# A block inversion whose last level works on 64-row quadrants, and a sample-state product split over two 32-row groups

## What is computed

```python
a = jnp.where(strict, beta[..., :, None] * jnp.einsum('bnhid,bnhjd->bnhij', k, k) * decay, 0.0)
lhs = a + jnp.eye(CHUNK)
sol = lax.linalg.triangular_solve(lhs, rhs, left_side=True, lower=True, unit_diagonal=True)
...
s = gl_c[..., None, None] * s + jnp.einsum('bhcd,bhce->bhde', ko_c, u)
```

## Time and profile before

| | us |
|---|---|
| median of 3 runs (1190.07 to 1191.61) | 1191.23 |
| the profiled execution | 1191.59 |
| its span | 1189.5 |
| PE busy | 1148.7 (97%) |
| DVE, POOL, ACT busy | 726.2, 610.2, 518.5 |
| one phase of the loop (two successive starts of line 778: 297.87 and 374.17) | 76.30 |
| mean granted TensorE clock | 0.99 |

### The profile page before, as it was taken

How to read it: one execution, slowest core, us unless ns; L and a number is a source line. 1 busy time by engine, 2 the same in 40 slices (tenths; PEclk the granted TensorE clock), 3 DMA queues, 4 the chain that set the end, 5 groups by cost and what they waited for, 6 DMA issues and landing times.

```text
span 1189.5 us, 22147 instructions
## 1 busy us (share of the span) xinstructions
PE 1148.7 (97%) x8349; PEld 1096.0 (92%) x8349; DVE 726.2 (61%) x1064; ACT 518.5 (44%) x898; POOL 610.2 (51%) x480
## 2 busy tenths in 40 slices
PE   6789999999999999999999989999999999999996
PEld 5689989899899998999989979999999999999996
DVE  6678896886868868778683546764135215314735
ACT  6554545544445354553462576542133123213531
POOL 0338558386584764847657374332433433435841
PEclk9899999999999999999999999999999999999998
DMA  6211223112222122121321116212222222222212
GB/s 236 61 57 45 75 73 100 57 35 81 74 72 83 31 85 74 50 78 44 98 93 41 49 38 222 71 54 72 77 83 90 73 87 88 71 88 89 91 35 80
DMA packets 32519, 92.28 MB, mean 78 GB/s; under 512 B 4688, under 2 KB 12240, under 8 KB 32464
## 3 DMA queue, kind: packets, MB, share of 16 engines
q1 hardware_dynamic: 32464, 91.52, 23.7%
HBM read 82.99 MB, written 8.52 MB: 77 GB/s over the span
## 4 chain that ended last, share of the span: by engine, by line
PE 77%; DVE 11%; issue 6%; ACT 4%; POOL 1%; DMA 0%; DVEq 0%; SPq 0%; ACTq 0%; POOLq 0%
PE ps L529 29%; PE ps L558 23%; PE ps L567 6%; DVE work L1338 5%; PE ps L883 4%; DVE ps L1341 4%; PE ps L716 2%; PE ps L696 2%; PE ps L711 2%; PE ps L770 1%; PE ps L778 1%; PE ps L744 1%; PE ps L577 1%; PE ps L590 1%; DVE o_a L1341 1%
## 5 line engine op out<-in xcount | busy, mean ns | idle before, releaser
L1812 POOL TENSOR_TENSOR w_lo<-raw,w_hi 128x1024 fp32r<-128x1024 f32 x123 | 298.6, 2429 | 380.3 <-ACT w_hi L981 225.8
L558 PE MATMUL ps<-in_hi,w_hi 128*128 128x288 f32 x992 | 305.7, 308 | 3.0 <-ACT work L1058 2.8
L558 PE MATMUL ps<-in_hi,w_lo 128*128 128x288 f32 x992 | 300.3, 303 | 0.0
L558 PE MATMUL ps<-in_lo,w_hi 128*128 128x288 f32 x992 | 299.0, 301 | 0.0
L558 PEld LDWEIGHTS ps<-in_hi,w_hi 128*128 128x128 f32 x992 | 188.9, 190 | 6.6 <-ACT w_hi L963 3.0
L558 PEld LDWEIGHTS ps<-in_hi,w_lo 128*128 128x128 f32 x992 | 188.9, 190 | 2.0
L558 PEld LDWEIGHTS ps<-in_lo,w_hi 128*128 128x128 f32 x992 | 188.8, 190 | 1.2
L1341 DVE SCALAR_TENSOR_TENSOR ps<-work,ct,ps 128x512 f32<-128x512 f32 x240 | 180.7, 753 | 7.4 <-DVE work L1460 1.7
L981 ACT CAST w_hi<-raw 128x1024 fp32r<-128x1024 f32 x61 | 63.8, 1047 | 224.3 <-PE ps L529 224.3
L1338 DVE TENSOR_TENSOR f_tmp<-f_tmp 128x576 f32<-128x576 f32 x31 | 70.7, 2282 | 96.4 <-ACT f_tmp L1288 91.0
L1338 DVE TENSOR_TENSOR o_a<-o_a,ps 128x576 f32<-128x576 f32 (+1 forms) x40 | 25.3, 634 | 144.7 <-PE ps L529 122.8
(11 more groups left out here) (290 smaller groups left out, 2396.0 us busy)
## 6 DMA issues: line engine op xcount, KB each, us to landing
raw<-w_all_in SPq DMA_DIRECT2D x136, 512.0 KB, 3.6
work<-s_in_in SPq DMA_DIRECT2D x8, 512.0 KB, 3.6
s_sample_out<-work SPq DMA_DIRECT2D x8, 512.0 KB, 2.7
xt<-x_t_in SPq DMA_DIRECT2D x4, 576.0 KB, 6.4
xt<-x_t_in SPq DMA_DIRECT2D x2, 1152.0 KB, 7.5
y_out<-o_a SPq DMA_DIRECT2D x16, 144.0 KB, 1.7
halo<-halos_in SPq DMA_DIRECT2D x9, 156.0 KB, 3.4
conf_rows_out<-c_rows SPq DMA_DIRECT2D x8, 135.0 KB, 2.2
```

Source lines behind the costliest of these rows:

```text
L558: t = mm(dense_ps(n, j, h), a[:, w, k], b[:, k, h * HALF:(h + 1) * HALF], start=r == 0, stop=r == PASS_MM // 2 - 1)
L1812: return gp.tensor_tensor(out, a, b, op)
```

## The change

The last level (l = 7) joins two 64-wide blocks of a 128-wide chunk. After the change only the quadrants that are not zero are computed:
- x: 4 matmuls of 64 weight columns and 64 moving columns over rows 0 to 63 (upper right quadrant of c, upper left of t). ACT copies the result, 64 partitions by 256 elements, to partitions 64 to 127 of `x_r`.
- u^T x and x^T u: 4 and 4 matmuls of the same size over rows 64 to 127. DVE writes the negated first result to a quadrant of `t_r` that was zero, and subtracts the second from the one quadrant of `u_r`.
- POOL copies one quadrant of the matrix to `c_r` instead of multiplying the whole with a mask.
- A `nop` on PE carries the waits ahead of the small groups, one on POOL ahead of its copy.

For the sample states `um` becomes 64x512, row r keeping the column block of sequence r // 8 mod 4. The two matmuls contract over rows 0 to 31 and 32 to 63, each into its own PSUM bank.

```diff
+        def quad(ap, i, j):
+            return ap[i * HP:(i + 1) * HP, 0:SEQ].rearrange("p (a b) -> p a b", a=TILES)[:, :, j * HP:(j + 1) * HP]
+
+        def sub(ap, c, i, j):
+            return ap[i * HP:(i + 1) * HP, c * P + j * HP:c * P + (j + 1) * HP]
...
+                        if l == LEVELS:
+                            pe.nop(nofuse=True)
                         for c in range(TILES):
-                            r = mm(tile(g(0), c), tile(w, c), tile(t, c),
-                                   start=True, stop=True)
+                            if l == LEVELS:
+                                r = mm(sub(g(0), c, 0, 0), sub(w, c, 0, 1), sub(t, c, 0, 0), start=True, stop=True)
+                            else:
+                                r = mm(tile(g(0), c), tile(w, c), tile(t, c), start=True, stop=True)
...
+                        if l == LEVELS:
+                            pe.nop(nofuse=True)
                         if l <= LEVELS:
                             for c in range(TILES):
-                                r = mm(tile(g(0), c), tile(u_r, c), tile(x_r, c), start=True, stop=True)
+                                if l == LEVELS:
+                                    r = mm(sub(g(0), c, 0, 0), sub(u_r, c, 1, 1), sub(x_r, c, 1, 0),
+                                           start=True, stop=True)
+                                else:
+                                    r = mm(tile(g(0), c), tile(u_r, c), tile(x_r, c), start=True, stop=True)
...
                         for c in range(TILES):
-                            r = mm(tile(g(1), c), tile(x_r, c), tile(u_r, c), start=True, stop=True)
+                            if l == LEVELS:
+                                r = mm(sub(g(1), c, 0, 1), sub(x_r, c, 1, 0), sub(u_r, c, 1, 1),
+                                       start=True, stop=True)
+                            else:
+                                r = mm(tile(g(1), c), tile(x_r, c), tile(u_r, c), start=True, stop=True)
...
                         for q in range(2):
-                            r = mm(g(q), smw(v["ko"]), v["um"][0:SMP, q * SEQ:(q + 1) * SEQ],
+                            rows = slice(q * SMP // 2, (q + 1) * SMP // 2)
+                            r = mm(g(q), v["ko"][rows, SEQ:SEQ + P], v["um"][rows, 0:SEQ],
                                    start=True, stop=True)
...
-                        r = A(x_r[:], g(0), ACT.Copy)
+                        if l == LEVELS:
+                            r = A(quad(x_r, 1, 0), quad(g(0), 0, 0), ACT.Copy)
+                        else:
+                            r = A(x_r[:], g(0), ACT.Copy)
...
-                        r = tt(t_r[:], t_r.bitcast(F32)[:, :], g(0), ALU.subtract)
+                        if l == LEVELS:
+                            r = ve.tensor_scalar(quad(t_r, 1, 0), quad(g(0), 0, 0), -1.0, None, ALU.mult)
+                        else:
+                            r = tt(t_r[:], t_r.bitcast(F32)[:, :], g(0), ALU.subtract)
...
-                    r = tt(dst, u_r.bitcast(F32)[:, :], g(1), ALU.subtract)
+                    if l == LEVELS:
+                        r = tt(quad(u_r, 0, 1), quad(u_r.bitcast(F32), 0, 1), quad(g(1), 0, 1), ALU.subtract)
+                    else:
+                        r = tt(dst, u_r.bitcast(F32)[:, :], g(1), ALU.subtract)
...
+                elif l == LEVELS:
+                    pool.nop(nofuse=True)
+                    r = gp.tensor_copy(quad(cr, 0, 1), quad(v["at"], 0, 1))
                 else:
                     r = tt(pr(cr), pr(v["at"]), lvl(l), ALU.mult)
...
-                        tt(v["um"][0:SMP, :].rearrange("p (q c) -> p q c", q=NS),
-                           smw(v["u"]).unsqueeze(1).to_broadcast([SMP, NS, P]),
-                           con("rowm", SMP).unsqueeze(2).to_broadcast([SMP, NS, P]),
+                        tt(v["um"][0:SMP, 0:SEQ].rearrange("p (q c) -> p q c", q=NS // 2),
+                           smw(v["u"]).unsqueeze(1).to_broadcast([SMP, NS // 2, P]),
+                           con("rowm", SMP).unsqueeze(2).to_broadcast([SMP, NS // 2, P]),
                            ALU.mult).then_inc(um_ready, 1)
...
-    put("rowm", np.arange(SMP)[:, None] // LS == np.arange(NS)[None, :])
+    put("rowm", np.arange(SMP)[:, None] // LS % (NS // 2) == np.arange(NS // 2)[None, :])
```

More of the change, by code:

```diff
@@ L32 @@
 P = 128
+HP = P // 2
 D = 1024
@@ L82 @@
            ("eps", 1), ("eps128", 1), ("big", P), ("big_s", SMP), ("lvl", LEVELS * P),
-           ("lvl_s", LEVELS_S * SMP), ("strict", P), ("rowm", NS)]
+           ("lvl_s", LEVELS_S * SMP), ("strict", P), ("rowm", NS // 2)]
 OFF, _o = {}, 0
```

## The result

| | before | after |
|---|---|---|
| median of all runs, us (12 each) | 1191.98 | 1185.44 |
| profiled execution's span, us | 1189.5 | 1182.2 |
| states of one phase to those of the next (372.49 less 297.01, before 374.17 less 297.87) | 76.30 | 75.48 |

The ratio of the times is 0.9950, 95% interval 0.9937 to 0.9964: **6.0 us faster**, between 4.3 and 7.5. I had said 3.6.

The account below looks back on a forecast made before the run. PE was taken as the bound, busy 1148.7 of 1189.5 us. Level 7 -0.2, states -3.0 and last head -0.4 sum to -3.6 us: 1188.0 against the profiled execution, 1187.6 as a median, range 1186.8 to 1191.2.

Parts of the forecast that it names:

- Bound by PE, and the saving reaches the end: Heads: PE and DVE both released by line 778, both start 0.43 us sooner, wait at line 684 unchanged.
- Level 7 nets nothing: Level 7: x group 0.07 to 0.12 us slower, slot 19 0.10 to 0.15 faster; -0.2 us over 8 heads.
- The switch: Level 7: leaving the full array for small matmuls and returning costs 0.30 to 0.35 us.
- The rival in which the 64-wide weights load no faster: Level 7: the 12 small matmuls keep 0.11 us spacing, costing +4.8 us; chance 0.05 as the slower rival.
- the slower case: Level 7's small matmuls keep 0.11 us spacing and the state halves queue: +4.4 us, 1195.6; chance 0.05.
- The states: Sample states: second matmul's first record beside the first's second, three spacings for four, 0.43 us a head.
- Seven heads: The sample-state gain of 0.43 us counts in seven heads, -3.0 us (0 to -3.0), lost in the last.
- The last head: Last head: half the `um` spreading saves POOL about 0.9 us, shortening PE's wait; -0.4 us (0 to -0.9).
- the level at +0.2: Level 7's term at the slow end of its bounds, -0.6 to +0.2 us over 8 heads.
- the case without overlap: Sample states: the two halves queue, only -0.2 and -0.4 us remain, 1190.6 us; chance 0.24.

Follow-up runs that it names:

- both halves in one row group: Changed kernel with both sample-state matmuls contracting over rows 0 to 31, rows 32 to 63 left out: 1.91 us to the sum, phase 76.26 us.
- level 7 alone: Changed kernel with the old sample states put back, level 7 still in quadrants: ratio 1.0009 (1.0000 to 1.0019), phase 76.27 us.
- second spreading: Changed kernel with POOL spreading the samples a second time in the last head only: PE waits 2.64 us at one new place, 1.00 at the old.

## Why the prediction was right or wrong

**Bound by PE, and the saving reaches the end: right.** The phase fell by 0.82 us of the 0.85 that the states lost; the wait ahead of line 684 rose from 0.43 to 0.49. DVE moved along, as its 1.53 us of idle time had promised.

**Level 7 nets nothing: right.** x group 0.81 (said 0.78 to 0.83), slot 19 1.04 (said 1.00 to 1.05), alone 1.0009. Inside the groups the small matmuls start 0.058 us apart; the forecast had 0.055, but its reading of the earlier trace rows came out right by luck: the pair's two records start 0.107 us apart, which is one step and not two, so the pair gives 0.11 a step and says nothing for the halving. What carried is the other argument, that the weight load sets the spacing and that half the columns halve it; 0.058 for 0.11 agrees. The switch, 0.32 us in both places (0.81 less 0.26 less 4 x 0.058, and 1.04 less 0.26 less 8 x 0.058), lies in the 0.30 to 0.35 that was allowed. The rival in which the 64-wide weights load no faster is out, and with it the slower case.

**The states: the term that was mis-sized.** The failed step reads "its first record may run beside the first matmul's second: three spacings instead of four". It is two: 0.85 us instead of 0.43. I had taken a float32 matmul's two records for two instructions in one queue and added the rule of program order to it. The records of the first and the second matmul start together, twice. The trace of before had nothing on this, and I had named 0.43 "full" overlap as the upper bound, when nothing in the rows excludes that two of the four records lie wholly beside the other two, which takes away 2 spacings, 0.86. The expected distance of 1.48 us to line 577 is 1.06, and DVE's idle time 0.69 instead of the 1.1 expected.

**Seven heads: one too many.** Between phases 1 and 2 nothing arrives; I had read DVE's idle time in one phase of the loop and taken it for phase 1, whose taps are written out differently. With both corrected, and the last head at 0.7, the sum is 6 x 0.83 + 0.7 = 5.7 us; measured 6.0 (4.3 to 7.5).

**The last head: right in its path, low in its size.** Said 0.4 (0 to 0.9), by way of POOL and not of PE; with the clock alike it was 0.67 or 0.83, and doubling POOL's part showed the path.

**Two sums are off.** With the level at +0.2 and nothing from the last head the forecast comes to 1188.4, not 1188.6, and the case without overlap to 1191.4, not 1191.2. Neither changes where the measured 1185.4 lies. It lies below the range because the range's lower end, 1186.8, still took 0.43 a head as the most the states could give.

## What to carry to other kernels

Two matmuls over 32 rows each ran wholly beside each other from different row groups, into different banks (one bank was not tried), and that was worth far more than making matmuls smaller, which pays only when the way to the small size and back (here 0.3 us, against 0.05 us that each smaller matmul saves) is shared by enough of them: some six, by that estimate. Bound an untried overlap by all the records that could lie side by side, not by an assumed order. And before a gain is multiplied by the number of heads, look at the unrolled first and last one by themselves.

## What the runs showed of the hardware that was not expected

Matmuls of different row groups left the program order: of four matmuls issued first, first, second, second, the third started 0.014 us after the first.

A DVE addition of two tensors in SBUF took 0.75 us alone and 1.95 us beside POOL's products, POOL's growing from 1.4 to 1.9; but in six profiles one addition took 5.0 to 6.0 us while three or four POOL products in a row ran at 1.4. Which of the two ways came went with the clock just before: with the low stretch behind the 2.5 us wait and the schedule untouched no addition took more than 2.2. With one addition moved to an earlier slot one took 4.8 in spite of it. Why is not shown.

Stretches at the lower clock (1.2 GHz) fell differently from profile to profile, and what one cost depended on what PE met next. Behind the wait of 1.0 us one came in six of the twelve profiles and cost 1.5 us: from the states of head 7 to those of the last head it is 103.15 us with it and 101.63 without (both halves in one row group, level 7 alone). Behind the wait of 2.5 us one came in six as well, delayed the last head's states by 1.5 us, and cost nothing at the output projection (15.03 against 15.18), where PE otherwise waited longer. In two profiles (level 7 alone, second spreading) one came behind the wait before the output projection instead, and the rest of the kernel took 474.5 us and not 473.1. A single pair of profiles can err by more than the smaller effects here.
